# Spreading a norm's factor by four narrow products, finishing a down projection bank by bank, and splitting two blocks ahead of a norm

## The reference

```python
def rmsnorm(x, g):
    return x * rsqrt(mean(x * x, axis=-1) + EPS) * g
# first block
a = rmsnorm(h, ln_pre_mix)
q, k, v, u, z = split(a @ w_in)
mixed = concat(rmsnorm(attn), rmsnorm(sgu)) @ w_out
h = h + rmsnorm(mixed, ln_post_mix)
f = rmsnorm(h, ln_pre_ffn)
g, up = split(f @ w_gate_up)
h = h + rmsnorm((silu(g) * up) @ w_down, ln_post_ffn)
h = h + sigmoid(h @ w_pe_gate + b) * (p @ w_pe_proj)
# second block, two layers (i = 0: stick breaking, i = 1: latent attention)
mod = silu(c) @ ada_w[i] + ada_b[i]          # sh1, sc1, g1, sh2, sc2, g2
x = x + g1 * mix(rms_norm(x, norm_mix[i]) * (1 + sc1) + sh1)
x = x + g2 * conv_ffn(rms_norm(x, norm_ffn[i]) * (1 + sc2) + sh2)
```

## Time and profile before

| | |
|---|---|
| median of 3 runs | 2192.85 us (2185.49 to 2193.33) |
| the profiled execution's own time | 2192.36 us |
| its span, first to last instruction | 2190.6 us |
| mean granted TensorE clock | 0.966 of 2.4 GHz |

### The profile page before, as it was taken

The page is one execution under the profiler, slowest core; times in us unless marked ns, Lnnn a source line. Parts: engine busy times, 40 slices in busy tenths (PEclk is TensorE's granted clock), DMA queues, the critical chain, the costliest instruction groups (busy, mean ns, idle before and its releaser), DMA issues.

```text
span 2190.6 us, 26879 instructions
## 1 busy us (share of the span) xinstructions
PE 2073.8 (95%) x9338; PEld 1654.1 (76%) x9346; DVE 1033.5 (47%) x1611; ACT 606.9 (28%) x1134; POOL 1215.6 (55%) x678
## 2 busy tenths in 40 slices
PE   5999889998998899898899999999999998999999
PEld 4876678886787677666788888878686677888887
DVE  4455479898225800465443333140865544333412
ACT  2225210001013320598221111121317733111210
POOL 6650558886564766433566666654351035666664
PEclk9999989999998899999999999988999999999999
DMA  6330248887231232100422333222120012323321
GB/s 230 125 115 1 77 145 286 286 287 262 77 98 55 77 96 92 44 1 13 141 87 96 96 96 96 96 68 68 48 79 29 1 49 77 96 96 96 96 96 67
DMA packets 62326, 221.15 MB, mean 101 GB/s; under 512 B 6912, under 2 KB 7168, under 8 KB 62128
## 3 DMA queue, kind: packets, MB, share of 16 engines
q1 hardware_dynamic: 44928, 161.25, 23.1%
q10 hardware_dynamic: 17328, 58.95, 7.6%
HBM read 218.03 MB, written 2.14 MB: 101 GB/s over the span
## 4 chain that ended last, share of the span: by engine, by line
PE 64%; DVE 5%; ACT 4%; issue 2%; DMA 0%; POOL 0%; ACTq 0%; DVEq 0%
PE bank L280 17%; PE bank L282 17%; PE bank L281 17%; PE bank L450 2%; PE bank L473 2%; PE bank L310 1%; PE bank L315 1%; PE bank L311 1%; PE bank L585 1%; ACT y L655 1%; PE bank L462 1%; ACT L663 1%; PE bank L381 1%; DVE big L1527 1%; DVE square_sum L734 1%
## 5 line engine op out<-in xcount | busy, mean ns | idle before, releaser
L280 PE MATMUL bank<-a_hi,w_hi 128*128 128x512 f32 x2072 | 814.0, 393 | 9.8 <-DVE a_lo L809 4.4
L282 PE MATMUL bank<-a_hi,w_lo 128*128 128x512 f32 x2072 | 809.1, 390 | 0.0
L281 PE MATMUL bank<-a_lo,w_hi 128*128 128x512 f32 x2072 | 809.1, 390 | 0.0
L854 POOL TENSOR_SCALAR w_hi<-raw 128x1024 fp32r<-128x1024 f32 x299 | 356.9, 1194 | 781.7 <-PE bank L282 498.1
L856 POOL TENSOR_TENSOR w_lo<-raw,w_hi 128x1024 fp32r<-128x1024 f32 x299 | 764.8, 2558 | 24.9
L280 PEld LDWEIGHTS bank<-a_hi,w_hi 128*128 128x128 f32 x2072 | 391.0, 189 | 93.7 <-POOL w_lo L856 5.4
L281 PEld LDWEIGHTS bank<-a_lo,w_hi 128*128 128x128 f32 x2072 | 390.9, 189 | 82.1 <-issue 0.7
L282 PEld LDWEIGHTS bank<-a_hi,w_lo 128*128 128x128 f32 x2072 | 390.7, 189 | 81.7
L1331 DVE CUSTOM_DVE_ANT_0 y<-y,cond 128x1024 f32<-128x1024 f32 x96 | 212.7, 2268 | 0.8 <-DMA y<-in_ada 0.8
L1342 DVE SCALAR_TENSOR_TENSOR tmp<-bank,vecs,tmp 128x511 f32<-128x511 f32 x88 | 66.0, 750 | 263.2 <-ACT tmp L1090 263.2
L809 DVE TENSOR_TENSOR a_lo<-big,a_hi 128x512 fp32r<-128x512 f32 x63 | 67.0, 1075 | 224.6 <-ACT a_hi L804 224.6
(11 more groups left out here) (207 smaller groups left out, 2369.0 us busy)
## 6 DMA issues: line engine op xcount, KB each, us to landing
raw<-in_stream SPq DMA_DIRECT2D x299, 512.0 KB, 3.5
y<-in_ada ACTq DMA_DIRECT2D x96, 512.0 KB, 4.7
x<-in_x SPq DMA_DIRECT2D x4, 512.0 KB, 6.7
bias<-in_bias ACTq DMA_DIRECT2D x1, 2048.0 KB, 14.1
y<-rel_rows ACTq DMA_DIRECT2D x1, 2048.0 KB, 9.2
bias<-rel_rows ACTq DMA_DIRECT2D x1, 2048.0 KB, 14.1
out<-x SPq DMA_DIRECT2D x8, 256.0 KB, 2.1
cond<-in_c ACTq DMA_DIRECT2D x1, 512.0 KB, 9.1
```

What stands on the lines that cost most here:

```text
L280: pe.matmul(o, lhs_hi, rhs_hi, start=start, stop=False, **kw)
L281: pe.matmul(o, lhs_hi, rhs_lo, start=False, stop=False, **kw)
L282: return pe.matmul(o, lhs_lo, rhs_hi, start=False, stop=stop, **kw)
L854: pool.tensor_scalar(w_hi[:, s, :], raw[:, j, :], 1.0, 1.0, ALU.mult, ALU.mult).then_inc(high_ready, 1)
```

## The change

Three edits go together. The spread no longer uses a diagonal matrix: TensorE takes the 128x1 column of factors of each token group, repeated 128 times, as weights, and the identity as moving operand, four products of 128 columns in place of one of 512; it waits for the inverse's last step. In `pe_down` the last two blocks are done bank by bank, six matmuls a bank, and a third sum group comes between the banks. GpSimd splits two instead of four blocks of the next phase ahead of the low parts of `pre_mix`, `pre_ffn`, `mix0`, `ffn0`, `mix1` and `ffn1`, and the other two behind them; the boundary at `out2` stays at four.

```diff
+AHEAD = 2
-        diag = sb("diag", [P, TT, P])
+        def pe_spread_rows(pe):
+            for t in range(TT):
+                m = pe.matmul(rstd_bank[:, t * P:(t + 1) * P], rms[:, 1, t:t + 1].broadcast_to([P, P]), ident, start=True, stop=True)
+            return m
         def pe_spread(pe, name):
-            pe.wait_ge(diag_ready, NORM_INDEX[name] + 1)
-            pe.matmul(rstd_bank[:], ones, diag[:].rearrange("p t i -> p (t i)"), start=True, stop=True).then_inc(rstd_ready, 1)
+            pe.wait_ge(inverse_step, 5 * inverse_index(name) + 5)
+            pe_spread_rows(pe).then_inc(rstd_ready, 1)
...
-            for i in range(FC // 4 * 4, FC):
-                chunk(i % 4, i, stop=i == FC - 1)
+            last = range(FC // 4 * 4, FC)
+            for i in last:
+                pe.wait_ge(split_ready, START[name] + 1 + i)
+                pe.wait_ge(lo_ready, LOW_AT[name] + 1 + i)
+            for c in range(DC):
+                for i in last:
+                    s, j = (START[name] + i) % SPLIT, i % 4
+                    m = pe_three_passes(pe, bank[c][:], w_hi[:, s, c * P:(c + 1) * P], w_lo[:, s, c * P:(c + 1) * P],
+                                        a_hi[:, j, :], a_lo[:, j, :], False, i == FC - 1, skip_group_check=True)
+                    if c == DC - 1:
+                        m.then_inc(block_done, 1)
+                if c < DC - 1:
+                    m.then_inc(down_done, 1)
+                if norm and c in (3, 5, 7):
+                    pe_sum_group(pe, norm, c // 2 - 1)
...
             dve_inverse(v, rms, sum_columns(name), P * NORM_CHUNKS[name], (rms_ready, s + 1), inverse_index(name))
-            dve_write_diag(v).then_inc(diag_ready, 1)
...
-            for b in range(SPLIT):
+            for b in range(AHEAD):
                 split(b, b, b, 0, wait=False)
             pool_lows("pre_mix")
-            split_stream(SPLIT, START["gu1"] + SPLIT)
+            for b in range(AHEAD, SPLIT):
+                split(b, b, b, 0, wait=False)
+            split_stream(SPLIT, START["gu1"] + AHEAD)
             pool_lows("pre_ffn")
-            split_stream(START["gu1"] + SPLIT, START["bq"] + SPLIT)
+            split_stream(START["gu1"] + AHEAD, START["bq"] + AHEAD)
...
-            split_stream(START["out2"] + SPLIT, START["gu2"] + SPLIT)
+            split_stream(START["out2"] + SPLIT, START["gu2"] + AHEAD)
             pool_lows("ffn0")
-            split_stream(START["gu2"] + SPLIT, START["qi"] + SPLIT)
+            split_stream(START["gu2"] + AHEAD, START["qi"] + AHEAD)
             pool_lows("mix1")
-            split_stream(START["qi"] + SPLIT, START["gu3"] + SPLIT)
+            split_stream(START["qi"] + AHEAD, START["gu3"] + AHEAD)
             pool_lows("ffn1")
-            split_stream(START["gu3"] + SPLIT, N_BLOCKS)
+            split_stream(START["gu3"] + AHEAD, N_BLOCKS)
```

More of the change, by code:

```diff
@@ L236, in two_blocks @@
         sq_ready, sq_added, group_used = sem("sq_ready"), sem("sq_added"), sem("group_used")
-        rms_ready, inverse_step, diag_ready, rstd_ready = sem("rms_ready"), sem("inverse_step"), sem("diag_ready"), sem("rstd_ready")
+        rms_ready, inverse_step, rstd_ready = sem("rms_ready"), sem("inverse_step"), sem("rstd_ready")
         scaled_ready, hi_ready, lo_ready, lo_pool_ready = sem("scaled_ready"), sem("hi_ready"), sem("lo_ready"), sem("lo_pool_ready")
@@ L254, in two_blocks @@
         qsq_ready, qsum_ready, qrms_ready = sem("qsq_ready"), sem("qsum_ready"), sem("qrms_ready")
-        k_diag_ready, k_rstd_ready, k_scaled = sem("k_diag_ready"), sem("k_rstd_ready"), sem("k_scaled")
+        k_rstd_ready, k_scaled = sem("k_rstd_ready"), sem("k_scaled")
         lat_split, uv_ready, selected, top_step = sem("lat_split"), sem("uv_ready"), sem("selected"), sem("top_step")
@@ L395, in pe_down, with chunk @@
         def pe_down(pe, name, n, norm=None):
-            def chunk(j, i, start=False, stop=False):
+            def chunk(j, i, start=False):
                 hi, lo = (first_hi, first_lo) if start else (a_hi[:, j, :], a_lo[:, j, :])
@@ L407, in chunk @@
                     m = pe_three_passes(pe, bank[c][:], w_hi[:, s, c * P:(c + 1) * P], w_lo[:, s, c * P:(c + 1) * P],
[L408 to L411, removed]
+                                        hi, lo, start, False, skip_group_check=True)
+                    if c == (3 if start else DC - 1):
                         m.then_inc(block_done, 1)
-                    if stop and norm and c in (5, 7):
-                        pe_sum_group(pe, norm, c // 2 - 2)
             for j in range(4):
@@ L738, in dve_add_squares @@
                 dve_add_square(v, name, c)
-        def dve_write_diag(v):
-            return v.tensor_tensor(diag[:], ident.unsqueeze(1).broadcast_to([P, TT, P]),
-                                   rms[:, 1, :].unsqueeze(2).broadcast_to([P, TT, P]), ALU.mult)
         def write_low(e, sem_done, split, c, shift=None, first=0):
@@ L876, in _ @@
             pool.wait_ge(zeroed, 2)
-            for b in range(SPLIT):
+            for b in range(AHEAD):
                 split(b, b, b, 0, wait=False)
             pool_lows("pre_mix")
-            split_stream(SPLIT, START["gu1"] + SPLIT)
+            for b in range(AHEAD, SPLIT):
+                split(b, b, b, 0, wait=False)
+            split_stream(SPLIT, START["gu1"] + AHEAD)
             pool_lows("pre_ffn")
-            split_stream(START["gu1"] + SPLIT, START["bq"] + SPLIT)
+            split_stream(START["gu1"] + AHEAD, START["bq"] + AHEAD)
             pool.wait_ge(x_ready, X_AT["pe_gate"] + DC)
-            pool.wait_ge(split_ready, START["bq"] + SPLIT)
+            pool.wait_ge(split_ready, START["bq"] + AHEAD)
             pool.memset(big[64:P, 0:B_HEADS:2, :], 0.0).then_inc(zeroed, 1)
@@ L891, in _ @@
             pool_lows("mix0")
-            split_stream(START["bq"] + SPLIT, START["out2"] + SPLIT)
+            split_stream(START["bq"] + AHEAD, START["out2"] + SPLIT)
             for h in range(B_HEADS):
@@ L954, in _ @@
             pe_down(pe, "down1", 0, norm="post_ffn")
-            for g in range(2, 5):
+            for g in range(3, 5):
                 pe_sum_group(pe, "post_ffn", g)
@@ L987, in _ @@
             pe_down(pe, "down2", 1, norm="mix1")
-            pe_norm(pe, "mix1", 2)
+            pe_norm(pe, "mix1", 3)
             pe_tiles(pe, "qi", "mix1")
@@ L1023, in _ @@
                 if i == 1:
-                    pe.wait_ge(k_diag_ready, 1)
-                    pe.matmul(rstd_bank[:], ones, diag[:].rearrange("p t i -> p (t i)"), start=True, stop=True).then_inc(k_rstd_ready, 1)
+                    pe.wait_ge(inverse_step, 5 * 9 + 5)
+                    pe_spread_rows(pe).then_inc(k_rstd_ready, 1)
                 head_sum(i)
@@ L1548, in _ @@
             dve_inverse(v, rms, head_sums[:, 0:TT], D_LAT, (qrms_ready, 1), 9)
-            dve_write_diag(v).then_inc(k_diag_ready, 1)
             v.wait_ge(lat_split, 2)
```

## The result

Four executions of the changed kernel took 2173.1 to 2173.8 us, median 2173.27, beside 2191.84 for the kernel before, run with it: ratio 0.992 (95% interval 0.9901 to 0.9938). Forecast were 2176.5 us and a range of 2166 to 2187. The profiled execution has a span of 2172.0 us against 2190.6, 18.6 less.

A forecast was written before the change was run, and what follows sets the result against it. TensorE, busy 95% of the span, was taken as the bound, with its waits at the norms as target. Terms 8.5 + 7.7 + 3.8 - 4 = 16.0 us off gave 2176.5 us, range 2166 to 2187.

The forecast's parts named there:

- The spread: At the norms, TensorE spreads factors without VectorE's diagonal matrix: 8.5 us gained over seven waited-for spreads.
- The 0.72 us of the diagonal: At each spread on the path, TensorE starts straight after VectorE's last small step, 0.72 us earlier.
- The 0.2 us for cheaper passes: At each low-clock spread, eight narrow passes take 1.87 us instead of 2.08 for two wide ones, 0.2 us less.
- Rival C: At seven spreads, narrow passes are dearer, 3.9 us instead of 1.87: time 2190.7, or 2183.6 at half; chance 0.07.
- a spread of under 2 us at the low clock: Sign at the spreads: VectorE's diagonal gone, eight passes in 1.8 to 2.0 us at the low clock.
- 5.5 at six places and 3.0 at `pre_mix`: Spread gain: 0.92 us at each of six norms, 5.5 us, and 3.0 us at pre_mix, whose diagonal took 2.73 us.
- GpSimd's order: Two splits ahead of the low parts: 3.5 us at pre_mix, 2.5 mix0, 1.1 post_mix, 0.6 ffn0 and ffn1; 7.7 us.
- No third block was late: Forecast charged 0 for third blocks split after the low parts; its rival had them late, 3 us, time 2179.5, chance 0.10.
- gu1: In the gate/up loop, GpSimd starts one split behind: 4 us charged, its first wait near the 22nd block.
- Rivals D: In gu1, GpSimd never catches up, all turns at 12.24 us: +20.8 instead of +4, time 2193.3; chance 0.08.
- E: In gu1, VectorE's turn stays at 12.95 us for 21 turns: +35.7 us, time 2208.5, slower than before; chance 0.05.
- The tails: Ends of down1 and down2, bank by bank: 2.0 and 1.8 us, 3.8 gained; sign 16.2 to 16.7 us to the inverse.

The follow-up runs named there:

- the spread alone with the wait: Kernel before with only the spread edit, plus GpSimd's split in down1 held until VectorE has written the gains: 2177.20 us, ratio 0.9947.
- The second profile of the same code: Traced execution of the unedited changed kernel, run again on another chip; that run's median was 2167.02 us, ratio 0.9901.
- the first comparison: The changed kernel run beside the kernel before: median 2173.27 us, ratio 0.992.
- the third: The changed kernel, unedited, run again on another chip beside the kernel before: median 2167.02 us, ratio 0.9901.
- the kernel with the wait: Changed kernel with GpSimd's split from down1's fourth block on held until VectorE has written the gains: 2163.75 us, ratio 0.9878.
- the kernel with the extra products and two blocks ahead: Changed kernel, split held until the gains are written, plus 20 and 24 unread constant products around five norms: 2167.66 us, ratio 0.9897.

## Why the prediction was right, and where not

By place, us gained in the profiled execution, from the starts of the same instructions in both timelines:

| place | forecast | measured |
|---|---|---|
| `pre_mix` (spread and order) | 6.5 | 6.4 |
| `sgu`, `attn`, clock in `out1` | 0 | 2.2 |
| `post_mix`, `pre_ffn`, first pair | 2.9 | 3.0 |
| `gu1` and the turn to `down1` | -4 | -1.9 |
| end of `down1` | 2.0 | 2.6 |
| `pe_proj`, `pe_gate` (clock) | 0 | -1.5 |
| `mix0` | 3.4 | 5.4 |
| `ffn0` | 1.2 | 1.1 |
| end of `down2` | 1.8 | 1.3 |
| `mix1` | 0.9 | 0.9 |
| attention of layer 2 (clock) | 0 | -1.3 |
| `ffn1` | 1.2 | 1.4 |
| `gu3` (clock) | 0 | -1.1 |
| sum (of unrounded terms) | 16.0 | 18.5 |

The total is nearer than its terms. Where the table is above the forecast it is by 7.1 us in all, where it is below by 4.6.

**The spread.** The 0.72 us of the diagonal is right: TensorE's wait fell from 2.02 or more to 1.29 or 1.30 us at six places. The 0.2 us for cheaper passes is not right: eight narrow passes take 2.07 or 2.08 us at the low clock, not 1.87, and 1.05 at the full one, where two wide took 1.02. The one-column products of the earlier trace rows were a bad stand-in for the load. Rival C is out, and so is a spread of under 2 us at the low clock: the edit costs nothing and gives nothing on TensorE. The figures of the Trainium skill for narrow and wide products ("TensorE: Matmul & The Clock Gate", Back-to-back issue gap), by which seven spreads would have given 2.7 us back, are not borne out: the difference here is 0.03 us a spread. The split of the gain into 5.5 at six places and 3.0 at `pre_mix` was wrong in its form: in the profile of the spread alone with the wait `pre_mix` gave 0.3 us and the six places 3.9. What the times have beyond that (5 to 8 us against some 4.5) is not settled; it lies within their intervals, and the low-clock stretches near 57 and 220 are of its size.

**GpSimd's order.** `pre_mix` and the short steps came as forecast. `mix0` gave 2 us more: 2.6 by the add (2.5 forecast), 1.3 since the last sums ran at full clock (2.29 us for two groups), and the rest behind them. No third block was late, but only since the clock was low: with the clock up it was, by 1.33 to 1.38 us.

**gu1.** GpSimd's first wait came at the 22nd block, counted from 1, as forecast (16th before the change), and the distance grew by 2.1 us, not by 4: the mechanism is right, the size half. The second profile of the same code has 238.4 us as well, but its first wait at the 18th block. Seen with its start the price is nothing: with two or with four blocks ahead the times are 0.3 us apart, for what the earlier start gains the longer recovery takes. Rivals D and E did not occur.

**The tails.** 3.9 us measured, 3.8 forecast. Of the two, 15.7 us lies under the 16.2 to 16.7 that were named as the sign, 17.1 above. What the step missed is that the released splits fall on the inverse, which cost 2.6 us at `mix1` when the edit stood alone.

**What no step saw.** The waits around the gains are set by whether GpSimd's split starts before or behind VectorE's shortest operations. The changed kernel lost 4.67 us there in the profiled execution of the first comparison and 0.89 in that of the third, and the times of the two comparisons, 2173 and mostly 2166 to 2169, fit that. The earlier trace rows show neither; the chain through `down1`'s first low parts was never read, because the change did not touch it. That the forecast lies 3.2 us from the time and not 9.5 (5 by the ratios) thus owes something to luck, to which of the two was hit; the lower edge of the range, 2166, just holds the other. The table's rows for clock come to -1.7 us together, with the 2.2 of `out1` counted in; why the clock moved there was only read from traces, not tried.

## What to carry to other kernels

A short VectorE operation that starts behind a long GpSimd one can cost what is left of the GpSimd operation, not its own 0.2 us, as the gains did here. So look for the chains of short steps on the path and hold GpSimd back over them with one wait, where its work has time (6.4 us in the kernel before, 5 to 9 in the changed one by the ratios). Where a kernel waits in short holes, cheap products in them can bring TensorE's clock back sooner, but only pay once what fed the slow pair is fast enough for the quick one. With two blocks ahead such products gave next to nothing at the norms, and the kernel was 3.9 us slower by a loss elsewhere; with three blocks ahead and fewer products it was 6.1 us faster. And profile the same code twice before believing a step of 1 to 2 us in a difference of profiles, and look first whether the granted clock differs at that spot.

## What was not expected of the hardware

- Eight float32 products of 128 columns, each with its own load, take as long as two of 512: 1.05 against 1.02 us at full clock, 2.08 against 2.08 at the low one.
- Even VectorE's one-input copy of 8 columns takes 2.14 us instead of 0.17 beneath a split: the copy into `mods` at 520.36 in the kernel with the wait ends at 522.50, and GpSimd's w_lo, begun at 519.22, at 522.47.
- Products of two bfloat16 constants with 128 columns stood in waits of 1.3 and 1.7 us at five norms. With 20 and 24 of them the granted clock over the first 4 us of the pair was 1.00 instead of 0.50 at all five, with 12 and 24 at four (0.78 at `ffn1`). Over nine of the ten spreads it was still 0.50.
- A busy TensorE can have the low clock: from 1478 to 1490 in the kernel with the wait it is busy for all of the 12 us, at first with products of 8 columns, and the granted clock is 0.50. In the kernel with the extra products and two blocks ahead this stretch came earlier and ended later, from 1473 to 1493, which cost it 3.3 us; another 1.2 us went to the low clock near 1514. Why it moved was not tried.
